# Two DRAM-to-DRAM copies move from SyncE's queue to ScalarE's, and an adding DMA of GpSimd moves behind two low parts

## The reference, cut to what matters

```python
mix = concatenate([attn_o, conv_o])
h = x + mix @ w_out                       # output projection, x is read again here
hn = rms_norm(h, norm_ffn_g)
y = h + (silu(hn @ w_gate) * (hn @ w_up)) @ w_down
```

## Time and profile before

| | us |
|---|---|
| median of 3 runs (1226.62 to 1227.45) | 1227.04 |
| the profiled execution | 1227.83 |
| its span, from the first to the last instruction | 1226.0 |
| TensorE busy in it | 1198.8 (98%) |
| VectorE busy | 721.7 (59%) |
| ScalarE busy | 442.0 (36%) |
| GpSimd busy | 522.6 (43%) |

### The profile page before, as it was taken

The page is one execution under the profiler, slowest core; times in us unless marked ns, Lnnn a source line. Parts: engine busy times, 40 slices in busy tenths (PEclk is TensorE's granted clock), DMA queues, the critical chain, the costliest instruction groups (busy, mean ns, idle before and its releaser), DMA issues.

```text
span 1226.0 us, 22971 instructions
## 1 busy us (share of the span) xinstructions
PE 1198.8 (98%) x9221; PEld 1136.3 (93%) x9221; DVE 721.7 (59%) x1190; ACT 442.0 (36%) x844; POOL 522.6 (43%) x442
## 2 busy tenths in 40 slices
PE   7999999999999979999999999999999999999998
PEld 7998779889877779999999999999999999999998
DVE  7888314414677612379548566656664179756665
ACT  6111120000487701255433333434343334345452
POOL 3446023233244424041886687768777740000020
PEclk9999999999999989999999999999999999999999
DMA  5488575343556596113322535443434687222223
GB/s 212 149 291 266 224 265 217 138 172 124 178 121 163 148 348 147 18 36 142 127 101 71 128 79 132 132 113 82 119 105 105 254 351 254 88 95 95 81 77 107
DMA packets 78697, 185.54 MB, mean 151 GB/s; under 512 B 7232, under 2 KB 24320, under 8 KB 76032
## 3 DMA queue, kind: packets, MB, share of 16 engines
q1 hardware_dynamic: 71088, 169.38, 39.7%
q0 software_dynamic: 7360, 14.42, 7.7%
q10 hardware_dynamic: 144, 0.27, 0.1%
HBM read 150.75 MB, written 59.25 MB: 171 GB/s over the span
## 4 chain that ended last, share of the span: by engine, by line
PE 34%; POOL 11%; issue 3%; DVE 3%; DMA 2%; ACT 1%; DVEq 0%; ACTq 0%
POOL w_lo L979 7%; PE ps L1651 6%; PE ps L1652 6%; PE ps L1653 6%; PE ps L1600 4%; PE ps L1602 4%; PE ps L1601 4%; DMA raw<-in_w 2%; POOL w_stage L1022 1%; POOL t_d L921 1%; POOL evac L1016 1%; ACT w_hi L1729 1%; PE ps L1625 1%; POOL norms L1016 1%; PE ps L1626 1%
## 5 line engine op out<-in xcount | busy, mean ns | idle before, releaser
L1138 PE MATMUL ps<-act_hi,w_hi 128*128 128x352 f32 x480 | 158.0, 329 | 8.0 <-DVE act_lo L2316 8.0
L1600 PE MATMUL ps<-combo,w_hi 128*128 128x264 f32 x560 | 159.7, 285 | 0.8 <-ACT evac L1729 0.4
L1601 PE MATMUL ps<-combo,w_hi 128*128 128x264 f32 x560 | 159.2, 284 | 0.0
L1602 PE MATMUL ps<-combo,w_lo 128*128 128x264 f32 x560 | 159.2, 284 | 0.0
L1140 PE MATMUL ps<-act_hi,w_lo 128*128 128x352 f32 x480 | 155.4, 324 | 0.0
L1139 PE MATMUL ps<-act_lo,w_hi 128*128 128x352 f32 x480 | 155.3, 324 | 0.0
L1651 PE MATMUL ps<-hid,w_hi 128*128 128x264 f32 x536 | 153.0, 285 | 0.0
L1652 PE MATMUL ps<-hid,w_hi 128*128 128x264 f32 x536 | 152.6, 285 | 0.0
L1653 PE MATMUL ps<-hid,w_lo 128*128 128x264 f32 x536 | 152.6, 285 | 0.0
L1600 PEld LDWEIGHTS ps<-combo,w_hi 128*128 128x128 f32 x560 | 105.4, 188 | 1.2 <-issue 0.6
L1602 PEld LDWEIGHTS ps<-combo,w_lo 128*128 128x128 f32 x560 | 105.5, 188 | 0.0
(11 more groups left out here) (479 smaller groups left out, 3494.4 us busy)
## 6 DMA issues: line engine op xcount, KB each, us to landing
w_stage<-in_w SPq DMA_DIRECT2D x55, 512.0 KB, 4.5
resid<-in_state_k SPq DMA_DIRECT2D x8, 1792.0 KB, 10.5
t_d<-in_w POOLq DMA_DIRECT2D x15, 768.0 KB, 8.3
h_d<-evac SPq DMA_DIRECT2D x37, 264.0 KB, 2.1
v_buf<-in_state_v SPq DMA_DIRECT2D x9, 1024.0 KB, 6.7
resid<-in_xT SPq DMA_DIRECT2D x16, 528.0 KB, 11.7
late<-h_d SPq DMA_DIRECT2D x6, 1056.0 KB, 12.8
raw<-in_w SPq DMA_DIRECT2D x12, 512.0 KB, 6.4
```

The costliest lines, as they stand in the source:

```text
L1138: pe.matmul(out, hi, rhs_hi, start=first, stop=False)
L1600: pe.matmul(out, hi[:, wk], x_hi[:, k, tk], start=(k == 0 and first), stop=False, skip_group_check=not first)
L1601: pe.matmul(out, hi[:, wk], x_lo[:, k, tk], start=False, stop=False, skip_group_check=not first)
L1602: mm = pe.matmul(out, lo[:, wk], x_hi[:, k, tk], start=False, stop=(k == 3), skip_group_check=not first)
```

## The change

The two copies P6 and P4 leave SyncE's queue, with their wait for P5's adds. They go out from ScalarE's queue instead, P4 first, right behind the square of job 3 of the output projection. In a pair, GpSimd's first adding DMA moves from behind the low part of (0, "P7") to behind that of (0, "P5"), past the low parts of A4 and P5. In the first pair its wait for eight adds moves with it.

```diff
@@ block.sync @@
             sp.dma_start(sums_blocks("P7"), down_blocks(0, 1)).then_inc(sums_copied, 16)
-            sp.wait_ge(sums_added, 16 * 4)
-            for product in ("P6", "P4"):
-                sp.dma_start(sums_blocks(product), sums_blocks("P5")).then_inc(sums_copied, 16)
@@ block.gpsimd @@
                 for x, product in PAIR_ORDER[6:]:
                     weight_low(a + x, product)
-                    if (x, product) == (0, "P7"):
+                    if (x, product) == (0, "P5"):
                         if part == 0:
                             pool.wait_ge(sums_added, 16 * 8)
@@ block.scalar, square(j) @@
                 act.activation(ps[:, 5, 0:QC], res[:, n, quarter(c)], ACT.Square).then_inc(h_sq, 1)
+                if j == 3:
+                    act.wait_ge(sums_added, 16 * 4)
+                    for product in ("P4", "P6"):
+                        act.dma_start(sums_blocks(product), sums_blocks("P5")).then_inc(sums_copied, 16)
```

## The result

The changed kernel takes 1212.36 us as the median of four runs (1211.71 to 1212.57), the kernel before 1226.83 us beside it: a ratio of 0.988, with a 95% interval of 0.9863 to 0.9897. That is 14.5 us gained where 16.3 were forecast. The profiled execution took 1212.29 us around a span of 1210.5, so the spans of the two profiles differ by 15.5.

A forecast was written before the change was run, and what follows sets the result against it. TensorE, 98% busy, was taken to bound the kernel, so only time out of its own sequence counts. The median 1227.04 less 10.0 (output projection) and 6.3 (pairs) gave 1210.7 us, range 1208.5 to 1219.

The forecast's parts named there:

- both places: TensorE's wait for x in the output projection (9.99 us) and its waits at A4 of the pairs (6.3 us).
- Part A: Output projection: copies issued by ScalarE after job 3's square, so x reloads 8.9 us earlier; gain 9.99 us, low end 8.8.
- the slack: Output projection: copies may land later before TensorE waits for OUT0+7 at job 20; 9.8 us, the smaller slack.
- By that rule the new queue gives x nothing: Copies against x's reload: queues share 16 DMA engines, so the gain is all in the later time of issue.
- so the terms are taken off the median unchanged: Sum: the profiled 1227.83 us was 0.8 above the median of 1227.04, so gains were subtracted from the median directly.
- Part B: Pairs: moving the adding DMA behind P5's low part lets VectorE's sum finish before TensorE's A4; gain 6.3 us, bounds 0 and 6.3.
- a gap in which VectorE gets in: Pairs: GpSimd's 0.8 us issue after P5's low part lets VectorE finish its sum, needing 0.55 us.
- I find nothing that would take them back: TensorE's sequence: it waits nowhere else after both gains, so the whole 10.0 and 6.3 us should show.
- The first (no gap): Pairs: VectorE is kept out or misses the gap, so moving the adding DMA brings nothing; 1217.0 us, chance 0.16.
- second: Output projection: x or the copies land late, TensorE stalls 5 us for OUT0+7 with 36 us copies; 1215.7 us, chance 0.12.
- third: Output projection: copies crawl on ScalarE's queue, delaying the splits of OUT0+6 and OUT0+7; slower, 1245.9 us, chance 0.05.
- The fourth: SyncE stays held at `conv_tail`, x comes as late as before and the pairs gain nothing; 1227.0 us, chance 0.05.

The follow-up runs named there:

- part A alone: The kernel after with the first adding DMA of a pair back behind the low part of (0, "P7"): 1217.93 us, ratio 0.9928.
- the two parts alone: Besides part A alone: the kernel before with only a pair's first adding DMA moved behind the low part of (0, "P5"), 1221.22 us, ratio 0.9956.
- Queue or time: The kernel before with the two copies on SyncE behind the reload of x, 1217.48 us, or on ScalarE at their old time, 1217.3 us.
- A4's run: The kernel after with the first adding DMA of a pair behind the low part of A4, one low part earlier: 1217.29 us, ratio 0.9913.
- behind A3: The kernel after with the first adding DMA of a pair behind the low part of A3, two low parts ahead of A4: 1217.75 us, ratio 0.993.

## Why the prediction was right, and where it was off

- **What bounds the kernel: right.** Only TensorE's own sequence mattered, both places were the right ones, and their waits are gone.
- **Part A, mechanism: right, with one sentence on it wrong.** First reload at 426.63 (I had 426.8), the square of job 3 over at 442.6 (442.5), no wait before job 4, clock 1.00. GpSimd's first P4 add is at 467.35 where I had 464, because the copies took 24.1 us and not 21.3, and the slack is 7.2 us where I had 9.8. "By that rule the new queue gives x nothing" failed as a reading of the rule: with the copies on ScalarE's queue at their old time the whole gain of part A was there (9.0 us), so either half of part A would have done.
- **Part A, size: too large.** The term was 9.99 us from one profile; three profiles give 8.4 to 10, and the three kernels that have this gain alone measure 8.4, 8.8 and 9.0 us by the medians. The sentence that failed is "so the terms are taken off the median unchanged": the profiled execution was 1.0 us above the median of 1226.83. The second profile of the kernel before took 0.7 us less than the first, and 0.5 of that lies in this place.
- **Part B, the order of steps: right.** A4's low part first, the sum at 1.8 us, p5 in time, period 39.4 us.
- **Part B, the reason: wrong in one step, so that its gain was in part luck.** I took the issue as a gap in which VectorE gets in, and the number of low parts as what kept it out. The end of the pair's other sum (L2810 in the earlier trace rows) fits as well with what the later runs show: VectorE gets in at the end of the low part that is running, if no issue stands ahead of that part in the run. The change worked because P5's low part is no longer behind the issue, not because the issue is behind P5. Behind A4, with the same issue moved one place, the reasoning of the forecast would have promised the same gain, and that kernel loses nearly all of it (a span of 1216.0 us, against 1216.7 with part A alone).
- **Part B, size: 5.1 to 5.4 us alone where 6.3 were forecast.** The missing 0.9 to 1.2 is about the new wait at B4, 1.13 us idle in that profile, with 0.3 of restart. On top of part A the span is 6.2 us shorter (1216.7 against 1210.5), which is the forecast: the wait at B4 stands in both of these profiles, 0.61 and 0.63 us, so it is paid once and doesn't belong to B alone. "I find nothing that would take them back" was the step that missed it. The load of the next pair's weights, beside the second adding DMA, was only just in time before: B4 of pair 1 started 16.96 us behind A4, where 16.78 do in the kernel with the second adding DMA later. It took 6.4 us before, and 6.5 to 7.1 in the profiles of the kernel after and of the two parts alone. I had followed GpSimd's queue, but not whose transfer the DMA runs beside. Why the wait is 0.28 us or none in the two kernels of "Queue or time" wasn't settled.
- **The rivals.** The first (no gap) didn't come about, though its doubt was well placed, as A4's run shows. The second and third have the right place and a real price, seen only when the copies are 20 us later; the wait is then for OUT0+6, and not for OUT0+7 as the second has it. The fourth didn't come about: SyncE was held at `conv_tail` for 0.36 us.

Of the 16.3 us, 14.5 came. The two profiles differ by 15.5, so 0.8 is missing between them, which is the wait at B4 (0.63, with 0.3 of restart). The other 1.0 is what the profiled execution of the kernel before lay above its median.

## What to carry to other kernels

A large transfer that nobody needs yet doesn't belong ahead of a small one in the same queue; put it behind, or on another queue, and ask who waits for its landing. A wait for a transfer can differ from one execution to the next (8.4 to 10 us here), so size it from more than one profile. Where GpSimd issues DMAs between its arithmetic, look at VectorE's instructions with two SBUF inputs in the run behind the issue. Place the issue one instruction further on than the one that VectorE waits for: right behind that one it cost nearly the whole gain of part B here. The end of a run does as well for VectorE, but brought the next issue too near here.

## What the runs showed of the hardware

- In the wake of the first adding DMA's issue GpSimd's low parts are recorded at 1.70 to 1.80 us and those without an issue ahead at 1.29, both with a spacing of 1.25 (behind the second one of pair 2 in the kernel after at 1.45), and VectorE's sum with two SBUF inputs is shut out until the last of them is done, or until GpSimd waits for something: 4.2 us behind A3, 4.25 in the kernel before, 5.5 when it arrives during the issue. With no issue ahead it gets its turn after one low part (1.76 us), and GpSimd's next one then waits about 0.46. The page "SBUF — State Buffer" of the Trainium skill, section "SBUF: two separate sides", gives the shared ports to whichever instruction starts first, for the whole of it: by that VectorE would have waited for one low part. The runs without an issue ahead agree (1.76 us), those in the wake of one don't. Why the wake differs was not settled; no run takes the issue apart.
- Where GpSimd reached an adding DMA (up to 768 KB) 5.3 to 6.1 us after the issue of the one before, it was held 1.1 to 3.7 us first (with the first adding DMA at the end of the run), and in the output projection of the kernel before 3.8 us when it reached one after 4.9; where it reached it 9.2 us or more after, it wasn't. What it waits for no run shows.
- Two DRAM-to-DRAM copies of 2816 KB took 19.8 to 24.1 us to land from ScalarE's queue behind the reload of x, 20.6 to 21.3 from SyncE's ahead of it and 27.3 behind it, and 31 from ScalarE's beside it. The next issue on SyncE's queue, of 36 KB, was held for 8.0 to 8.9 us.
